# Stick-breaking attention summed by parts: the scan's running products are turned and multiplied directly, with row differences of the values

## The reference

```python
z = einsum(q[:, :, q0:L], k[:, :, :L]) * scale
past = s_idx < t_idx
log_fail = where(past, log_sigmoid(-z), 0.0)
between = cumsum(log_fail, axis=3, reverse=True) - log_fail
w = where(past, exp(log_sigmoid(z) + between), 0.0)
out = einsum(w, v[:, :, :L])
```

## Time and profile before

| | |
|---|---|
| median of 3 runs | 1556.41 us (1555.81 to 1557.64) |
| the profiled execution | 1555.21 us |
| its span, first to last instruction | 1553.0 us |
| busy: PE, DVE, ACT, POOL | 93%, 66%, 57%, 12% of the span |
| units 0 to 7 of this attention | 311.14 to 456.47 us of the span |
| mean granted TensorE clock | 0.972 |

### The profile page before, as it was taken

The page is one execution under the profiler, slowest core; times in us unless marked ns, Lnnn a source line. Parts: engine busy times, 40 slices in busy tenths (PEclk is TensorE's granted clock), DMA queues, the critical chain, the costliest instruction groups (busy, mean ns, idle before and its releaser), DMA issues.

```text
span 1553.0 us, 21196 instructions
## 1 busy us (share of the span) xinstructions
PE 1438.6 (93%) x7417; PEld 1105.5 (71%) x7417; DVE 1019.5 (66%) x1832; ACT 888.5 (57%) x1599; POOL 184.6 (12%) x243
## 2 busy tenths in 40 slices
PE   6999999988889888999989999996999999999996
PEld 5888989443435544447868888885877888888885
DVE  4512126688759876757774333448788999889887
ACT  6321557577656565663433332342677887887776
POOL 0000000356540000000000000000111121111211
PEclk9999999999899999999999999996999999999998
DMA  6200125310020000102130100043897566666794
GB/s 217 58 9 33 59 108 211 129 70 1 1 83 27 1 1 28 55 28 82 55 122 1 55 28 28 28 163 132 307 364 249 203 209 217 223 215 218 236 356 151
DMA packets 87298, 184.80 MB, mean 119 GB/s; under 512 B 14272, under 2 KB 24512, under 8 KB 86464
## 3 DMA queue, kind: packets, MB, share of 16 engines
q1 hardware_dynamic: 77952, 161.90, 29.2%
q0 software_dynamic: 7200, 22.03, 5.5%
q10 hardware_dynamic: 2080, 0.01, 0.1%
HBM read 216.42 MB, written 26.21 MB: 156 GB/s over the span
## 4 chain that ended last, share of the span: by engine, by line
PE 68%; DVE 10%; DMA 9%; ACT 5%; issue 4%; POOL 2%; DVEq 0%; ACTq 0%; SPq 0%; POOLq 0%
PE psum L1875 25%; PE psum L2111 17%; DMA up_stage<-in_w_up 9%; PE psum L1859 8%; PE psum L2007 6%; PE psum L2030 4%; DVE up_rest L1541 4%; PE psum L1852 3%; PE psum L1989 3%; DVE gate_rest L1541 2%; POOL arena L750 2%; PE psum L2160 1%; ACT gate_high L1116 1%; PE psum L2256 1%; ACT arena L1234 1%
## 5 line engine op out<-in xcount | busy, mean ns | idle before, releaser
L2007 PE MATMUL psum<-arena 64*128 64x512 f32 (+7 forms) x384 | 119.4, 540 | 22.8 <-ACT arena L1087 14.5
L1541 DVE TENSOR_TENSOR down_rest<-down_stage,down_high 128x1024 fp32r<-128x1024 f32 x96 | 115.0, 1218 | 29.8 <-ACT down_high L1116 29.8
L1541 DVE TENSOR_TENSOR up_rest<-up_stage,up_high 128x1024 fp32r<-128x1024 f32 x100 | 117.0, 1219 | 16.4 <-ACT up_high L1116 16.0
L2030 PEld LDWEIGHTS psum<-ident,arena 128*128 128x128 f32 x576 | 70.1, 150 | 69.3 <-ACT arena L815 33.3
L1859 PE MATMUL psum<-arena 128*128 128x512 f32 (+2 forms) x352 | 118.6, 489 | 0.8 <-DVE arena L1409 0.8
L815 ACT ACTIVATE arena<-psum 128x512 f32<-128x512 f32 (+1 forms) x192 | 85.5, 502 | 55.5 <-PE psum L2030 55.1
L1875 PE MATMUL psum<-up_high,rows_high 128*128 128x256 f32 x384 | 110.3, 287 | 6.5 <-DVE up_rest L1541 6.1
L2007 PEld LDWEIGHTS psum<-arena 64*128 64x128 f32 (+1 forms) x384 | 49.5, 194 | 93.7 <-issue 47.2
L1541 DVE TENSOR_TENSOR gate_rest<-gate_stage,gate_high 128x1024 fp32r<-128x1024 f32 x100 | 115.7, 1217 | 0.4 <-ACT gate_high L1116 0.4
L1116 ACT ACTIVATE up_high<-up_stage 128x1024 fp32r<-128x1024 f32 x100 | 100.3, 1060 | 24.7 <-DMA up_stage<-in_w_up 24.7
L1417 DVE TENSOR_TENSOR_SCAN arena<-arena,singles 128x768 f32<-128x768 f32 (+7 forms) x64 | 90.7, 1416 | 29.9 <-POOL arena L750 29.8
(11 more groups left out here) (369 smaller groups left out, 3624.4 us busy)
## 6 DMA issues: line engine op xcount, KB each, us to landing
gate_stage<-in_w_gate SPq DMA_DIRECT2D x25, 2048.0 KB
up_stage<-in_w_up SPq DMA_DIRECT2D x25, 2048.0 KB
down_stage<-in_w_down SPq DMA_DIRECT2D x24, 2048.0 KB
arena<-in_x SPq DMA_DIRECT2D x16, 512.0 KB, 3.5
arena<-in_w_mkv SPq DMA_DIRECT2D x8, 1024.0 KB, 6.3
arena<-in_w_in SPq DMA_DIRECT2D x4, 1024.0 KB, 10.4
arena<-in_w_mo SPq DMA_DIRECT2D x4, 1024.0 KB, 6.4
mv_times_w_mo_spill<-arena SPq DMA_DIRECT2D x8, 512.0 KB, 2.8
```

What stands on the lines that cost most here:

```text
L1541: ins = dve.tensor_tensor(split[part][1][:, k, :], stage[part][:, k, :], split[part][0][:, k, :].bitcast(F32), ALU.subtract)
L2007: mm = pe.matmul(scores_of(kind, n)[:, at:end], lhs, rhs(at, end), start=True, stop=True)
L2030: mm = pe.transpose(dst[:, r * P:(r + 1) * P], rows(u, r, a)[:, j * P:(j + 1) * P], ident[:, :])
```

## The change

The products F are now what is turned and multiplied. ACT makes only the fail, with six buffers in place of three and three. POOL masks only it. DVE's scan writes straight into the buffers that PE turns, and the product with the take is gone. In exchange the values are replaced by the differences v(s-1) - v(s): SP moves the values by a row with DMAs inside the chip (after the load of group 2), and DVE subtracts, one tile of 128 rows after each copy of a key product. The last value of each tile is gathered into 8 rows, turned by PE in four small turns at the start of group 3, copied by ACT, and added by DVE when a unit is copied out of PSUM. The first output column is set to zero at the end.

```diff
@@ SP: the input loads
             for g in range(2, len(GROUPS)):
                 load_group(g)
+                if g == 2:
+                    sp.wait_ge(*copied(T - 1))
+                    sp.dma_start(v_ahead[1:P, :, :], v_sb[0:P - 1, :, :]).then_inc(s_va, 16)
+                    sp.dma_start(v_ahead[0:1, 1:T, :], v_sb[P - 1:P, 0:T - 1, :]).then_inc(s_va, 16)
+                    for t in range(T):
+                        sp.dma_start(v_last[t:t + 1, :], v_sb[P - 1:P, t, :]).then_inc(s_va, 16)
@@ POOL
-                for buf, full, masked, fill in ((f_sb, s_f, s_fm, 1.0), (g_sb, s_g, s_gm, 0.0)):
-                    block_ = buf[:, n % 3, t * P:(t + 1) * P]
-                    pool.wait_ge(full, n + 1)
-                    pool.affine_select(out=block_, in_=block_, compare_op=ALU.is_gt, fill=fill, base=0,
-                                       pattern=[[-1, P]], channel_multiplier=1).then_inc(masked, 1)
+                block_ = f_sb[:, n % FAILS, t * P:(t + 1) * P]
+                pool.wait_ge(s_f, n + 1)
+                pool.affine_select(out=block_, in_=block_, compare_op=ALU.is_gt, fill=1.0, base=0,
+                                   pattern=[[-1, P]], channel_multiplier=1).then_inc(s_fm, 1)
@@ ACT: take(n), FAILS = 6
-                if n >= 3:
-                    act.wait_ge(s_w, n - 2)
-                do(act.activation(f_sb[:, n % 3, 0:L], src, ACT.Sigmoid, scale=-(HD ** -0.5)), s_f)
-                do(act.activation(g_sb[:, n % 3, 0:L], src, ACT.Sigmoid, scale=HD ** -0.5), s_g)
+                if n >= FAILS:
+                    act.wait_ge(s_w, n - FAILS + 1)
+                do(act.activation(f_sb[:, n % FAILS, 0:L], src, ACT.Sigmoid, scale=-(HD ** -0.5)), s_f)
@@ DVE: the key products
                 taken(2, i, kT[:, i % 4, 512 * (i // 4):512 * (i // 4) + 512])
+                if i == 0:
+                    dve.wait_ge(s_va, 16 * (T + 2))
+                do(dve.tensor_tensor(v_sb[:, i, :], v_ahead[:, i, :], v_sb[:, i, :], ALU.subtract), s_vd)
@@ DVE: the rows
                 dve.wait_ge(s_fm, n + 1)
-                one(dve.tensor_tensor_scan(fall[:, a, SEQ - L:SEQ][:, ::-1], f_sb[:, n % 3, 0:L][:, ::-1],
-                                           tiny.to_broadcast([P, L]), 1.0, ALU.mult, ALU.add))
-                dve.wait_ge(s_gm, n + 1)
                 before_ = u - 1 if last_row("sb", r) else u - 2
                 if n == ROWS:
                     dve.wait_ge(s_pr, len(PRODUCTS))
                 if before_ >= 0:
                     dve.wait_ge(s_t, LAST["sb", before_] + 1)
-                do(dve.tensor_tensor(w_row(u, r, a)[:, 0:L], g_sb[:, n % 3, 0:L],
-                                     fall[:, a, SEQ - L + 1:SEQ + 1], ALU.mult), s_w)
+                do(dve.tensor_tensor_scan(w_row(u, r, a)[:, 0:L][:, ::-1], f_sb[:, n % FAILS, 0:L][:, ::-1],
+                                          tiny.to_broadcast([P, L]), 1.0, ALU.mult, ALU.add), s_w)
@@ DVE: out_rows
-                do(dve.tensor_copy(mixT[:, chunk0 + p, 512 * g:512 * (g + 1)], bank(6 + u % 2)), s_copied)
+                    do(dve.tensor_tensor(dst.rearrange("p (a b) -> p a b", a=GRP), src.rearrange("p (a b) -> p a b", a=GRP),
+                                         last, ALU.add), s_copied)
@@ PE: start of group 3
+            pe.wait_ge(s_va, 16 * (T + 2))
+            dst = begin(("last_values", 0, 0))
+            for p in range(PAIRS):
+                mm = pe.transpose(dst[:, p * T:(p + 1) * T], v_last[:, p * P:(p + 1) * P], ident[0:T, 0:T])
```

More of the change, by code:

```diff
@@ L128, in transposition_rounds @@
         add("x", t, "dve")
+    add("last_values", 0, "act", 1)
     for i in range(T):
@@ L244, in moe_layer @@
         cT = cut(45056, 5, SEQ)
-        f_sb = cut(0, 3, SEQ)
-        g_sb = cut(3072, 3, SEQ)
+        v_ahead = cut(45056, T, SBW)
+        v_last = cut(49152, SBW)[0:T, :]
+        v_lastT = junk[:, 512:512 + PAIRS * T].rearrange("p (a b) -> p a b", a=PAIRS)
+        FAILS = 6
+        f_sb = cut(0, FAILS, SEQ)
         def row_buffers(kind, first, second):
@@ L264, in moe_layer @@
         wT_sb = cut(6144, 4, 512)
-        fall = cut(23040, 2, SEQ + 1)
         mqT_h = cut(16384, HEADS, SEQ)
@@ L435, in moe_layer @@
         s_mk1 = sem("mem_k_reloaded")
-        s_qz = sem("scan_ends_made")
+        s_va = sem("values_moved_by_a_row")
+        s_vd = sem("value_differences_ready")
         s_pr = sem("projection_product")
@@ L440, in moe_layer @@
         s_f = sem("sb_fail_ready")
-        s_g = sem("sb_take_ready")
         s_fm = sem("sb_fail_masked")
-        s_gm = sem("sb_take_masked")
         s_w = sem("sb_weights_ready")
@@ L736, in _ @@
             do(pool.tensor_scalar(pad_row[:, :], tokf[:, 0:1], float(SEQ + 1), None, ALU.add))
+            do(pool.memset(v_ahead[0:1, 0, :], 0.0))
             do(pool.memset(tiny[:, :], 0.0), s_const)
-            pool.wait_ge(s_pr, FIRST_OF[MO])
-            for b in range(2):
-                pool.memset(fall[:, b, SEQ:SEQ + 1], 1.0).then_inc(s_qz, 1)
             for n in range(ROWS * N_UNITS):
@@ L923, in _ @@
             act.wait_ge(s_gain, 16 * GAINS)
+            empty(("last_values", 0, 0), v_lastT.rearrange("p a b -> p (a b)"), bank(ROUND["last_values", 0, 0] % 2)[:, 0:PAIRS * T])
             for i in range(T):
+                if i == 2:
+                    act.wait_ge(s_vd, T)
                 if i >= 2:
@@ L1408, in out_rows @@
                 dve.wait_ge(s_prod, prod_count(kind, u))
-                do(dve.tensor_copy(mixT[:, chunk0 + p, 512 * g:512 * (g + 1)], bank(6 + u % 2)), s_copied)
-            dve.wait_ge(s_qz, 2)
+                dst, src = mixT[:, chunk0 + p, 512 * g:512 * (g + 1)], bank(6 + u % 2)
+                if kind == "sb":
+                    last = v_lastT[:, p, GRP * g:GRP * g + GRP].unsqueeze(2).to_broadcast([P, GRP, P])
+                    do(dve.tensor_tensor(dst.rearrange("p (a b) -> p a b", a=GRP), src.rearrange("p (a b) -> p a b", a=GRP),
+                                         last, ALU.add), s_copied)
+                else:
+                    do(dve.tensor_copy(dst, src), s_copied)
+            dve.wait_ge(s_te["act"], EMPTIED[ROUND["last_values", 0, 0]][1])
             for n in range(ROWS * N_UNITS):
@@ L1432, in _ @@
                 out_rows("sb", u, s_pv, s_o, 0)
+            do.settle()
+            do(dve.memset(mixT[:, 0:PAIRS, 0:1], 0.0))
             def head_roots(t):
@@ L1927, in _ @@
                     project(g, i)
+            pe.wait_ge(s_va, 16 * (T + 2))
+            dst = begin(("last_values", 0, 0))
+            for p in range(PAIRS):
+                mm = pe.transpose(dst[:, p * T:(p + 1) * T], v_last[:, p * P:(p + 1) * P], ident[0:T, 0:T])
+            mm.then_inc(s_t, 1)
             for i in range(T):
@@ L2049, in _ @@
                 pe.wait_ge(*copied(m))
+            pe.wait_ge(s_vd, T)
             pe.wait_ge(s_te["act"], EMPTIED[ROUND[("mk", MT - 1, 1)]][1])
@@ L2058, in _ @@
             half_of = lambda a: slice(HD * a, HD * a + HD)
-            attention("sb", w_row, wT_sb, s_s, s_g, s_w, s_pv, s_o,
+            attention("sb", w_row, wT_sb, s_s, s_f, s_w, s_pv, s_o,
                       lambda p, a, t: (qT[half_of(a), p, t * P:(t + 1) * P], lambda b, e: kT[half_of(a), p, b:e]),
@@ L2064, in _ @@
             pe.wait_ge(s_o, N_UNITS)
-            pe.wait_ge(s_g, 8 * HEADS)
+            pe.wait_ge(s_f, 8 * HEADS)
             pe.wait_ge(s_wuq, 80)
```

## The result

| | before | after |
|---|---|---|
| median | 1556.78 us (1555.78 to 1560.13, 6 runs) | 1542.09 us (1536.56 to 1546.75, 6 runs) |
| ratio to before, 95% interval | | 0.9905 [0.9889, 0.9921] |
| the profiled execution, its span | 1555.21, 1553.0 | 1541.1, 1539.3 |
| the first attention, units 0 to 7 | 145.3 us | 115.2 us |
| its first scores start at | 274.25 us | 285.18 us |

The change makes the kernel 14.7 us faster; 25.3 were forecast. The place that the forecast was about did better than forecast, and a place that it priced at next to nothing, the move of the values in the projections, took 11 us back.

What follows compares the result with a forecast made beforehand. PE and DVE were both near their limit in long units, DVE the bound in short ones. Attention 145.3 to 117.8 us, 27.5 less, minus 0.5 added and 1.7 clock: 25.3 off 1556.41, 1531.1 us; forecast 1527 to 1537, 8-in-10 range 1524 to 1542.

Steps and rivals of the forecast that it cites:

- What is added: Projections: cost of moving values, subtractions and small turns; move lands in 11 us, 0.5 us in all on PE's path.
- some 35 us of slack: Projections: time the moved values have to spare before DVE's first subtraction at 120.1 us waits for them.
- The alarm: Ahead of group 3: PE waits if values land after some 150 us; gain eaten only at some 175.
- The attention: First attention, units 0 to 7: shortened from 145.3 to 117.8 us, 27.5 less.
- an allowance for masks: Units 4 to 6: masks formerly hidden behind products cost some gaps ahead of scans, 0.3 us per unit.
- That DVE's product was the bound: Attention units: PE waits 2.5 us for DVE's product in unit 1; removing products frees 8.2 us of DVE per long unit.
- The clock: Units 0 to 7: one half-clock stretch allowed, 1.7 us; ends are none or one in each unit.
- What comes behind this attention waits for nothing earlier than its end: Behind the first attention: its saving reaches the total unchanged, 25.3 us off 1556.41.
- Masks (1599): Attention: each DVE scan waits 1.8 us for a POOL mask, 42 us slower, 1599 us; chance 0.04.
- Waits that move instead of going (1547): Attention: PE's waits and slow clock stay, only 9.9 us less, 1547 us; chance of 1537 to 1550: 0.20.
- More than that (1524): Attention: shorter units, no slow stretch, 112.9 us, 32.4 less, 1524 us; chance of under 1527: 0.12.
- No gain: Attention: another 2.5 us wait per unit replaces that for DVE's product; 1553 to 1559 us, chance 0.03.

Runs made afterwards that it cites:

- experiment 3: Changed kernel with its move cut into 126 and 1 partitions: 1529.80 us; or into eight DMAs of 127 partitions, 2 KB each: 1538.50 us.
- Experiment 2: Kernel before with only the ten DMAs of the move added, their data unused: 1564.52 us, ratio 1.0071.
- experiment 4: Split kernel plus one DVE product per row into a buffer nobody reads: 1552.88 us, ratio 0.9999 to the kernel before.
- split kernel: Changed kernel with its 127-partition move cut into two DMAs of 112 and 15 partitions: 1527.17 us, ratio 0.9837 to the kernel before.
- experiment 8: Split kernel plus a second 128x128 POOL mask per row into a spare buffer: 1526.28 us, ratio 0.9833 to the kernel before.
- split_move_again: Split kernel unchanged, run once more on another chip: 1529.83 us, ratio 0.9832 to the kernel before.

## Why the prediction was right about the attention and short on the total

The time of 1542.09 sits at the upper edge of the range of 1524 to 1542, inside the band that the prediction gave to a rival (1537 to 1550) and not inside its own forecast of 1527 to 1537. It got there for neither reason: that the range held was luck.

*The step that failed* is "What is added", and in it one term: the move, priced at 11 us as four times a 512 KB DMA of 2.8 us, with "some 35 us of slack". Its last packet ended 87 us behind its issue, eight times the price. The earlier trace rows has 128 partitions by the kernel's code; its size was carried over, and its number of partitions, which decides (experiment 3), was not looked at. Sent as 112 + 15 partitions it takes 15.0 us, near the 11. The slack was there: DVE asked for the data at 119.0, 48 us behind the issue.

*The alarm was near in time and had the wrong path.* The prediction said that a landing later than about 150 us, 80 behind the issue, begins to hurt and that one at 175 would eat the gain, since PE needs the differences in group 3. PE did stop at 150.9, and the data at 159.5 cost 10.0 us of waiting and 3.0 of slow clock. But it stopped in group 2, not ahead of group 3. What failed is the list of those who stand behind the wait: DVE's 128x512 copies, which empty PE's banks, stand behind its first subtraction, and the next weights behind the move in SP's queue ("the next load behind them in SP's order waits for the query products anyway"). Experiment 2 shows that the second path alone costs 11 us.

*The attention*: 117.8 us forecast, 115.2 measured. Units 1 and 2 at 21.4 (20.95), unit 0 at 22.1 (21.65), unit 3 at 16.5 (16.70), units 4 to 6 at 10.0 (9.35), unit 7 at 6.4 (6.85). PE's wait at a unit's end, in place of 2.53, was put at 0.9 to 1.0 and is 0.82. The short units were 0.65 us too long in the forecast, 0.3 of it an allowance for masks; what the rest is wasn't looked for. DVE is busy 15.6 us in a long unit, not 16 to 17, and its long gaps are not masks.

*That DVE's product was the bound* is shown by experiment 4: alone it gives the whole gain back. ACT's second sigmoid is next. Alone it makes a long unit 24.05 us, with ACT busy only 19.20 of them and PE waiting for its sigmoids and copies again and again (1.07 us once, 0.27 to 0.48 at five places). PE itself is third (20.13 busy). The change had to take both away to reach 20.95; the prediction counted both, the sigmoid as 7 us of ACT. In the split kernel, with the serial move out of the way, the attention takes 118.1 us in its trace with two slow stretches and the whole change is worth 26.2 us, against 25.3 forecast.

*The clock*: 1.7 us were allowed in the attention and none were spent in this trace, though the split kernel's trace shows two stretches there. Elsewhere it took 3.0 us in the projections and, net of what the kernel before loses there, some 2 behind the attention. "What comes behind this attention waits for nothing earlier than its end, and I carry the difference over as it is" holds but for such stretches.

*The rivals.* Masks (1599): out, by the time itself and by experiment 8. Waits that move instead of going (1547): the time fell into its band, the mechanism is not there, with PE's waits in units 1 and 2 down to the one at the end and no slow stretch. More than that (1524): the attention went halfway there, from 117.8 to 115.2 with 112.9 as that case. No gain: out, 0.9905 [0.9889, 0.9921].

## What to carry to other kernels

Before a DMA is priced by its bytes, look at its count of partitions: a shift by one turns 128 into 127, and that goes through one engine; cut it so that 16, or a number near it, divides the large part (112 + 15 and 126 + 1 both did). When a wait is added, list everything that stands behind it on that engine and everything behind the DMA in its queue; slack for the data itself is not slack for them. Where two engines are each close to the bound, give each its old work back alone: that shows what each costs by itself, and the two prices need not add (25.7 and 11.3 us here, and some 24 together by the ratios).

## What the runs showed of the hardware that was not expected

- A DMA inside the chip from 127 partitions to 127 ran at 27 GB/s as 16 KB packets of 0.61 us, one in flight at a time, and its 112 + 15 partitions landed in 15.0 us. Of 126 partitions 14 packets were in flight. SP was held for 41.4 us at the next DMA; another load of 768 KB took 39.2 us to land beside the serial one, 5.7 in the split kernel.
- Neither whether the clock falls nor for how long follows from the pause ahead of it: behind 3.22 and 3.23 us of pause the stretches were 6.8 and 3.4. Behind PE's wait of 1.68 us ahead of unit 3 the clock fell in one trace of the split kernel (`split_move`) and stayed full in the other (`split_move_again`) and in the changed kernel's.
- With the product on DVE, giving ACT more work made units 1 and 2 shorter, 24.59 instead of 26.49 us for unit 1. That it is the clock, kept full as PE's one long wait became several short ones, is a reading of two traces and not tested.
- One kernel varies here by some 9 us from run to run (1522.92 to 1532.11 in 6 runs of the split kernel, 1549.09 to 1558.48 in 17 of the kernel before). Half-clock stretches that come and go are seen in the traces, and differences of 2 us could not be told by medians of 5 or 6.
